# Cast and subtract of each weight quarter in alternation on GpSimd, in a two-layer encoder at split fp32 precision

## The reference

```python
h = x @ w_in[l]                       # 1024 x 2048
oa = swa_sink_attention(...)          # 6 heads, window of chunks, one sink per head
ob = diff_attention(...)              # 6 heads, two maps of width 32 each, block-causal
oc = multiscale_pool(...)             # running means over 2, 4, 8, 16 tokens, then 64x64 products
x = layer_norm(ALPHA * x + concat(oa, ob, oc) @ w_o[l])
x = layer_norm(ALPHA * x + conv_gated_mlp(x, w_up[l], conv_w[l], conv_b[l], w_down[l]))
```

## Time and profile before

| | |
|---|---|
| Median of 3 runs | 2554.15 us (2548.34 to 2560.25) |
| The profiled execution's own time | 2556.16 us |
| Its span, first to last instruction | 2554.3 us |
| Mean granted TensorE clock | 0.969 of full speed |
| PE busy | 2382.2 us, 93% |
| POOL busy | 1673.2 us, 66% |
| DVE busy | 1493.0 us, 58% |
| ACT busy | 783.6 us, 31% |
| DMA traffic | 102 GB/s on average |

### The profile page before, as it was taken

One profiled execution on the slowest core, in us unless ns is written; L12 is line 12 of the kernel. 1 busy time (PEld: TensorE's weight loads), 2 busy tenths in 40 slices (PEclk: granted clock), 3 DMA queues, 4 the chain that ended last, 5 costly groups with the idle time before them and its releaser, 6 DMA issues.

```text
span 2554.3 us, 32182 instructions
## 1 busy us (share of the span) xinstructions
PE 2382.2 (93%) x11352; PEld 1971.3 (77%) x11352; DVE 1493.0 (58%) x2983; ACT 783.6 (31%) x1667; POOL 1673.2 (66%) x2884
## 2 busy tenths in 40 slices
PE   7988878999999998969999998989999998999997
PEld 5777766888887876758888776778888777888885
DVE  4347555665664596236666289236666656756557
ACT  1025204554452122115554022025545411222221
POOL 5743464556666796845666788765555577978874
PEclk8999988999999999979999999999999999999998
DMA  6633322333323232323332332343333122333332
GB/s 216 198 112 116 103 78 73 93 94 95 101 75 92 95 103 88 120 75 108 97 100 83 108 100 83 124 108 92 97 101 96 58 92 85 114 111 105 108 99 75
DMA packets 325583, 259.62 MB, mean 102 GB/s; under 512 B 37611, under 2 KB 274479, under 8 KB 325423
## 3 DMA queue, kind: packets, MB, share of 16 engines
q1 hardware_dynamic: 300096, 221.49, 28.5%
q10 hardware_dynamic: 25327, 36.07, 4.9%
HBM read 236.81 MB, written 20.71 MB: 101 GB/s over the span
## 4 chain that ended last, share of the span: by engine, by line
PE 74%; DVE 15%; POOL 4%; DMA 3%; ACT 2%; issue 2%; ACTq 0%; SPq 0%; DVEq 0%
PE psum L830 39%; PE psum L1068 13%; PE psum L856 6%; PE psum L953 5%; PE psum L886 3%; PE psum L909 3%; PE psum L940 2%; POOL w_lo L809 2%; DVE conv L1470 2%; DVE x_res L1682 1%; POOL w_hi L806 1%; DVE room L1340 1%; DVE conv L1448 1%; DVE mid L1636 1%; DMA w_raw<-in_w_in 1%
## 5 line engine op out<-in xcount | busy, mean ns | idle before, releaser
L806 POOL CAST w_hi<-w_raw 128x256 fp32r<-128x256 f32 x1440 | 579.9, 444 | 852.6 <-DMA w_raw<-in_w_up 467.3
L809 POOL TENSOR_TENSOR w_lo<-w_raw,w_hi 128x256 fp32r<-128x256 f32 x1440 | 1114.2, 804 | 0.0
L830 PE MATMUL psum<-x_hi,w_hi 128*128 128x512 f32 x1792 | 731.2, 408 | 35.4 <-POOL w_lo L809 17.0
L830 PE MATMUL psum<-x_lo,w_hi 128*128 128x512 f32 x1792 | 710.9, 397 | 0.0
L830 PE MATMUL psum<-x_hi,w_lo 128*128 128x512 f32 x1792 | 710.2, 396 | 0.0
L1068 PE MATMUL psum<-w_hi,hid 128*128 128x512 f32 x1408 | 446.3, 398 | 18.7 <-DVE x_res L1682 13.0
L830 PEld LDWEIGHTS psum<-x_hi,w_hi 128*128 128x128 f32 x1792 | 345.1, 193 | 114.6 <-POOL w_lo L809 22.0
L830 PEld LDWEIGHTS psum<-x_hi,w_lo 128*128 128x128 f32 x1792 | 344.0, 192 | 75.5
L830 PEld LDWEIGHTS psum<-x_lo,w_hi 128*128 128x128 f32 x1792 | 345.3, 193 | 68.7 <-issue 2.0
L1448 DVE SCALAR_TENSOR_TENSOR conv<-psum,prm_all,conv 128x511 f32<-128x511 f32 x176 | 131.8, 749 | 427.3 <-ACT conv L1257 427.0
L1068 PEld LDWEIGHTS psum<-w_hi,hid 128*128 128x128 f32 x1408 | 262.0, 190 | 77.3 <-DVE x_res L1682 15.1
(11 more groups left out here) (134 smaller groups left out, 2684.2 us busy)
## 6 DMA issues: line engine op xcount, KB each, us to landing
w_raw<-in_w_up SPq DMA_DIRECT2D x176, 512.0 KB, 3.7
w_raw<-in_w_down SPq DMA_DIRECT2D x88, 512.0 KB, 3.6
w_raw<-in_w_in SPq DMA_DIRECT2D x36, 512.0 KB, 4.0
w_raw<-in_w_o SPq DMA_DIRECT2D x32, 512.0 KB, 3.6
qk_scratch<-stage_qk SPq DMA_DIRECT2D x48, 256.0 KB, 3.3
q_stack<-qk_scratch ACTq DMA_DIRECT2D x72, 128.0 KB, 2.4
k_stack<-qk_scratch ACTq DMA_DIRECT2D x36, 256.0 KB, 3.4
w_raw<-in_w_in SPq DMA_DIRECT2D x16, 384.0 KB, 3.3
```

The costliest lines, as they stand in the source:

```text
L806: nc.gpsimd.tensor_copy(w_hi[:, slot, cut], w_raw[:, slot, cut]).then_inc(s["w_high"], 1)
L809: i = nc.gpsimd.tensor_tensor(w_lo[:, slot, cut], w_raw[:, slot, cut], w_hi[:, slot, cut].bitcast(F32), ALU.subtract)
L830: mm = nc.tensor.matmul(o, w, v[:, k, :], start=(k == 0 and w is wh and v is x_hi[h]), stop=(k == KT - 1 and w is wl))
```

## The change

POOL's two loops over the quarters become one. The number, the shapes and the operands of the instructions stay as they are, and so do the semaphores and the value that each wait waits for; only the order on POOL's queue changes, from C0 C1 C2 C3 S0 S1 S2 S3 to C0 S0 C1 S1 C2 S2 C3 S3 (C a cast, S a subtraction). The wait ahead of a subtraction is for the instruction just ahead of it.

```diff
                 cuts = [slice(c, c + 256) for c in range(0, 1024, 256)]
-                for cut in cuts:
+                for q, cut in enumerate(cuts):
                     nc.gpsimd.tensor_copy(w_hi[:, slot, cut], w_raw[:, slot, cut]).then_inc(s["w_high"], 1)
-                for q, cut in enumerate(cuts):
                     pool.wait_ge(s["w_high"], 4 * n + q + 1)
                     i = nc.gpsimd.tensor_tensor(w_lo[:, slot, cut], w_raw[:, slot, cut],
                                                 w_hi[:, slot, cut].bitcast(F32), ALU.subtract)
```

## The result

The median fell from 2555.5 us (20 runs, 2535.4 to 2575.4) to 2545.7 us (20 runs, 2536.8 to 2550.5): ratio 0.9967, 95% interval 0.9952 to 0.9982. I had forecast 2565.9 and a range from 2556: both miss, and the sign is wrong. The runs also lie closer together, within 14 us instead of 40.

The account below looks back on a forecast made before the run. PE was taken to bound the kernel, with POOL on its chain in 19 tiles. 7.0 + 3.0 + 1.7 = 11.7 us took the profiled 2556.16 to 2567.9, so the median to 2565.9 us; range 2556 to 2580.

Parts of the forecast that it names:

- What bounds the kernel: PE, busy 2382.2 of 2554.3 us; POOL, busy 66%, looks hidden but stands in the chain with 2% and 1%.
- 19 tiles' work of POOL on the chain: 19 of 360 tiles, where whole-tile projections and output products follow each other; PE starts 0.04 us after POOL in one.
- Joints and price x: POOL's overlaps between instructions, and wake-up x = 0.05 us ahead of each subtraction: a tile grows by 0.37 us to 4.6.
- The rival that the wait lays open the fixed part: On POOL, x = 0.15 us and a tile grows by 0.77: 26.3 us in sum, 2580; chance 0.20.
- Tiles on the chain and next to it: 19 x 0.37 = 7.0 us on PE's path, and 3.0 us at seven more places where PE follows POOL closely.
- the place at 2215.9: PE takes up the last of five pauseless POOL tiles 0.93 us later; 5 x 0.37 - 0.93 gives 0.9 us.
- The clock: PE's idle near 1454 grows to 2.5 us, giving one new stretch at the lower clock: 1.7 us.
- I cost everything else at nothing: The other 330-odd tiles, covered by PE's slack of 1 to over 10 us, and SP: no cost.
- the third rival: POOL's pauses of 0.05 let DVE in before the subtraction, some 8 us won, POOL's growth hidden: 2546; chance 0.08.
- the turn already passes at each joint: Argument against better turn-taking of DVE and POOL: four casts and four subtractions are the same eight turns in either order.
- a hidden cost: Rival: the loop of slot, DMA and POOL, or PE's wait on DVE, takes up POOL's growth: 2554 to 2559; chance 0.20.

Follow-up runs that it names:

- Experiment 6: The changed kernel with each cast also waiting for the subtraction before it, eight pauses a tile: 2578.2 us, ratio 1.0092 to the original.
- Experiment 1: Original order (four casts, four subtractions), but every subtraction waits for the tile's fourth cast, one pause a tile: 2543.1 us, ratio 0.9959 to the original.
- experiment 3: The new order with four pauses in feed-forward tiles (U, D) alone, other tiles as in the original kernel: 2531.6 us, ratio 0.9921.
- the repeat: Second run of the kernel with four pauses in U and D tiles alone, other tiles in the original order: 2536.9 us, ratio 0.9936 to the original.
- experiment 9: The new order with four pauses in tiles of the up product (U) alone, other tiles as in the original kernel: 2540.3 us, ratio 0.9945.
- experiment 5: Original order, but in U and D tiles alone every subtraction waits for the fourth cast, one pause a tile: 2537.1 us, ratio 0.9941 to the original.
- experiment 2: Original kernel's casts and subtractions alternated with casts one ahead (C0 C1 S0 C2 S1 C3 S2 S3), without a pause: 2554.1 us, ratio 0.9993.
- experiment 8: Original order, but in every second tile of all kinds subtractions wait for the fourth cast, one pause: 2540.8 us, ratio 0.9942 to the original.

## Why the prediction was wrong, point by point

**What bounds the kernel.** PE with 19 tiles' work of POOL on the chain was right. I read the chain for POOL alone and passed over the line beside it: L1470 stands in it with 5.72 us at 1131, for an instruction that other rows put at 0.68. A group whose longest instruction lasts eight times its median has a waiting partner, and DVE's partner in SBUF is the engine that the change touches.

**Joints and price x.** The mechanism held. I took x = 0.05 by POOL's other wake-ups; it measured 0.07 to 0.08. A tile grew by 0.48 instead of 0.37. The rival that the wait lays open the fixed part had priced x at 0.15 (2580); it stayed at half of that, though above the 0.065 from which I had let the rival decide. From start to start a tile of before took 4.11 us and not the 4.22 that I had added up, so the 4.59 of after met my 4.6 in part by luck.

**Tiles on the chain and next to it.** 7.0 + 3.0 us forecast; the two stretches that hold 15 of the 19 tiles lost 9.4 in the profiles, and PE's waits for POOL grew by 9.0 in the two groups shown. POOL's two lines went from 3% of the chain to 6%, where I had said 4. Experiment 6 confirms that this cost is real. At the place at 2215.9, where I had put 0.9, the same matmul did lose 0.8 us against 2182.4, with 0.68 of idle ahead of it until `w_lo` was ready; but by 2455.6 after had this back, so a delay at one place is not yet one at the end.

**The clock.** One stretch at the lower level did come where I had put it: PE idled 2.65 us ahead of 1446.7, and the granted clock was at its lower level for the next 3.4 us. But over the whole span of the two profiled executions the mean rose from 0.969 to 0.977, since stretches elsewhere fell away, and PE was busy 11.7 us less with the same matmuls: taken over the run, the term had the wrong sign.

**The step that failed** is "I cost everything else at nothing", and with it the argument against the third rival, that "the turn already passes at each joint". It doesn't always. With POOL in a long run of overlapping instructions there are joints at which DVE is not let in, up to the end of the run. The rival had the right mechanism, but I sized it at the norm's L1657 and L1658, which hardly changed (their means went from 1464 and 1442 ns to 1415 and 1416), gave it 0.08, and coupled it with a hidden cost. What happened is both. In the profiles, which lie 18.0 us apart, some 14 us were won around two starved products and some 9 lost on POOL; 6.2 came from the first 456 us (below), and 6.8 from the three stretches 1686 to 1958, 2003 to 2182 and 2456 to the end. The medians lie only 9.9 us apart, so the profiled pair overstates the gain.

**What stays open.** The first 456 us gave after 6.2 us, in which no starved L1470 lies. The granted clock of that stretch was 0.93 against 0.91 before. Experiment 1 was 5.3 us slower there and experiment 3 was 5.1 faster. In experiment 3 the first tile with pauses begins late:

```profile
345.23 0.40 POOL L807 CAST w_hi<-w_raw 128x256 fp32r<-128x256 f32 x1
```

Up to there POOL has the order of before, and yet PE was 3.1 us ahead of before (3.7 in the repeat, 1.0 in experiment 9, whose pauses begin at the same tile). So a difference of up to some 4 us arises there without any pause; how much of the 6.2 is of that kind, and what decides it, no run tells. And of the nine starved products in the profile of before two clearly cost PE time; that another execution has others there would explain the wide spread of its times, but only one execution of each kernel was profiled.

## What to carry to other kernels

Look at the longest instruction of a group, not at its mean: one at nine times the minimum, on DVE while GpSimd runs without a gap, may be a shut-out. Whether it costs shows when the starts of the same matmul are compared; the chain alone also named two that cost nothing. A gap of 0.08 us on GpSimd was enough to end one, and with one gap in every tile of 4 us none was seen, so put waits into long runs of GpSimd work, in the stages where GpSimd isn't on the path, and leave them out of those where PE waits for it: four pauses in the U and D tiles gave 0.6 to 0.8%, the same pauses everywhere 0.3%, and on the wrong tiles nothing or a loss. Few pauses did about as well as placed ones: one in every tile gave 0.4%, one in every second tile, wherever it fell, 0.6%. And tiles left without a pause stay open to it, as experiment 5 shows. An added wait is not only a cost to the engine that waits; ask who else is queued for what that engine holds.

## What the runs showed of the hardware that I had not expected

DVE and POOL hold each other up by whole instructions, which I knew from the earlier trace rows. The Trainium skill, SBUF — State Buffer, section SBUF: two separate sides, says the same: of a GpSimd instruction and a DVE instruction that has two inputs in SBUF or runs in a 2-port mode, whichever starts first has the shared pair of ports for the whole instruction, and the other is blocked. By that rule a DVE instruction would wait for one instruction of POOL, 0.74 us at most, and L1470 would last 1.42 at most. The trace agrees for most: of the 58 L1470 of before that began beside POOL, 46 lasted 1.34 us or less. Three lasted 1.57 to 1.76. It disagrees for nine, which waited through nine or ten instructions of POOL, and for the 8.84 us of experiment 5 and the 13.55 us of experiment 2, through some 25.

What opens this state was seen in part. In before, all nine began at least 13 instructions after POOL's last pause (16 that began sooner lasted 1.27 us at most), in experiment 8 two at the tenth, in experiment 5 one at the eleventh; with a pause in every tile (after, experiments 1 and 6) no instruction of DVE took over 0.6 us more than the shortest of its line and shape; and 33 that began beside POOL as late as the nine weren't starved. In experiment 8 a pause of 0.08 us closed it, and by experiments 1 and 2 it is the pause that counts and not the order of casts and subtractions. Why a joint of two overlapping instructions doesn't let DVE in after a long run, and does after a short one, no run here tells.
